# Expert blocks of 32 rows in four column quarters instead of 64 rows in two halves

## What is computed

```
expert_idx, gate_w = route(x2, w_router, router_bias)      # two experts of one group of four
h = silu(xb @ w1[e]) * (xb @ w3[e])                         # 1024 -> 512, xb: rows of expert e
y = h @ w2[e]                                               # 512 -> 1024
out[token] += gate * y                                      # summed over the token's two experts
```

## Time and profile before

| | us |
|---|---|
| runs | 3816.04, 3819.41, 3820.52 (median 3819.41) |
| profiled execution | 3819.16 |
| its span, first to last instruction | 3817.6 |
| TensorE matmuls busy | 3498.3 (92%), 15780 instructions |
| TensorE weight loads busy | 1803.3 (47%) |
| VectorE busy | 1159.3 (30%) |
| ScalarE busy | 757.9 (20%) |
| GpSimd busy | 177.0 (5%) |

### The profile page before, as it was taken

How to read it: one execution, slowest core, us unless ns; L and a number is a source line. 1 busy time by engine, 2 the same in 40 slices (tenths; PEclk the granted TensorE clock), 3 DMA queues, 4 the chain that set the end, 5 groups by cost and what they waited for, 6 DMA issues and landing times. The chain is left out here.

```text
span 3817.6 us, 47479 instructions
## 1 busy us (share of the span) xinstructions
PE 3498.3 (92%) x15780; PEld 1803.3 (47%) x15780; DVE 1159.3 (30%) x2400; ACT 757.9 (20%) x1418; POOL 177.0 (5%) x169
## 2 busy tenths in 40 slices
PE   8998998899969989997999679999998788899998
PEld 5445444555544454445555334444344577444443
DVE  1564112322333751113332320000446555410001
ACT  1134112223221151102222220000123422100000
POOL 1000002100020000003000110000000000000000
PEclk9999999899979999998999889999999887999999
DMA  7112223898231103234986212235121000122221
GB/s 280 56 45 78 77 77 132 324 389 353 77 130 66 56 23 112 76 133 153 420 336 268 81 57 77 77 83 143 67 76 54 1 0 0 44 77 77 77 77 66
DMA packets 79142, 457.64 MB, mean 120 GB/s; under 512 B 12160, under 2 KB 12296, under 8 KB 32112
## 3 DMA queue, kind: packets, MB, share of 16 engines
q1 hardware_dynamic: 42912, 310.40, 21.6%
q0 software_dynamic: 19776, 112.50, 8.3%
q10 hardware_dynamic: 16272, 32.43, 2.5%
HBM read 416.23 MB, written 39.06 MB: 119 GB/s over the span
## 5 line engine op out<-in xcount | busy, mean ns | idle before, releaser
L779 PE MATMUL pb<-arena,xT 128*64 x1984 | 445.6, 383 | 16.4 <-DVE streamed L1699 5.9
L779 PE MATMUL pb<-streamed,xT 128*64 128x256 f32 x1984 | 445.6, 383 | 0.0
L535 PE MATMUL pb<-xT,streamed 128*128 128x512 f32 x832 | 369.4, 603 | 0.0
L779 PEld LDWEIGHTS pb<-arena,xT 128*64 128x64 f32 x1984 | 267.8, 138 | 162.4 <-issue 31.6
L704 PE MATMUL pb<-xT,streamed 128*128 128x512 f32 x768 | 335.3, 595 | 2.6 <-ACT arena L1193 2.6
L888 PE MATMUL pb<-arena,streamed 128*128 128x512 f32 x704 | 306.4, 598 | 8.9 <-DMA streamed<-in_w_tail 7.2
L863 PE MATMUL pb<-xtok,streamed 128*128 128x512 f32 x704 | 305.0, 596 | 5.8 <-DVE xtok L1829 5.8
L863 PE MATMUL pb<-arena,streamed 128*128 128x512 f32 x704 | 304.2, 595 | 5.8 <-DVE arena L1829 5.8
L779 PEld LDWEIGHTS pb<-streamed,xT 128*64 128x64 f32 x1984 | 267.9, 138 | 0.0
L535 PEld LDWEIGHTS pb<-xT,streamed 128*128 128x128 f32 x832 | 159.9, 193 | 201.5 <-issue 201.4
L704 PEld LDWEIGHTS pb<-xT,streamed 128*128 128x128 f32 x768 | 146.4, 191 | 186.6 <-issue 186.6
(11 more groups left out here) (359 smaller groups left out, 3756.8 us busy)
## 6 DMA issues: line engine op xcount, KB each, us to landing
arena<-in_w_moe SPq DMA_DIRECT2D x128, 1024.0 KB, 11.7
streamed<-in_w_tail SPq DMA_DIRECT2D x87, 1024.0 KB, 4.8
streamed<-in_w_layer SPq DMA_DIRECT2D x78, 1024.0 KB, 4.9
arena<-in_w_moe POOLq DMA_DIRECT2D x64, 1024.0 KB, 9.7
ys_dram<-am ACTq DMA_DIRECT2D x120, 128.0 KB, 6.5
xT<-xs_dram ACTq DMA_DIRECT2D x26, 512.0 KB, 8.2
xs_dram<-lnw POOLq DMA_DIRECT2D x16, 512.0 KB, 20.5
lnw<-in_ln_par POOLq DMA_DIRECT2D x4, 1024.0 KB, 5.3
```

The lines of the kernel that those rows point to most:

```text
L535: last = mm(pb[bank][:, 0:cols], unit(w, u, k), rhs[:, k * cols:(k + 1) * cols], start=(k == 0), stop=(k == KC - 1))
L779: last = mm(pb[m][r0:r0 + MOE_BLOCK, 0:FW], rows, w, start=(k == 0), stop=(k == KC - 1))
```

## The change

MOE_BLOCK becomes 32. It follows that COLS = 4, FW = 128 and DW = 256 (columns of a part in up and down, before 256 and 512), N_BLK = (1024 + 16 * 31) // 32 = 47 and 12 tiles of four blocks in place of 16 of two. The relay buffers hold three of four parts, 3072 columns in place of 2048; w2's moves to another place. turn has one transpose in place of two. The three values per block become one, the expert's number, loaded ahead of silu (ScalarE) and of the hidden rows (VectorE); TensorE still loads its offset. One semaphore expert_here for each matrix replaces the two waits: SyncE and GpSimd wait for an expert's arrival and raise it. The copies of w1 and w3 no longer wait on up_ready themselves. The copy of the y block moves from VectorE to ScalarE, and its store is one DMA. TensorE's code is unchanged but for the sizes.

```diff
-MOE_BLOCK = 64
+MOE_BLOCK = 32
+STORES = 1
...
-        w2_relay = streamed[:, 2 * RELAY:3 * RELAY]
+        w2_relay = sr[:, 13312 - S - RELAY:13312 - S]
...
-        expert_loaded = [[sem(f"expert_loaded{q}_{p}") for p in range(PIECES // 2)] for q in range(2)]
+        expert_loaded = [sem(f"expert_loaded_{n}") for n in ("w1", "w3", "w2")]
+        expert_here = [sem(f"expert_here_{n}") for n in ("w1", "w3", "w2")]
...
-        def block_values(eng, b):
-            off = eng.value_load(blk_tab[0:1, b:b + 1], min_val=0, max_val=SLOT)
-            even = eng.value_load(blk_tab[0:1, N_BLK + b:N_BLK + b + 1], min_val=32, max_val=32 * N_EXP // 2)
-            odd = eng.value_load(blk_tab[0:1, 2 * N_BLK + b:2 * N_BLK + b + 1], min_val=32, max_val=32 * N_EXP // 2)
-            return off, even, odd
-        def wait_expert(eng, l, values, m):
-            for q in range(2):
-                eng.wait_ge(expert_loaded[q][m], l * (16 * N_EXP) + values[1 + q])
-                alone(eng)
+        def block_expert(eng, b):
+            return eng.value_load(blk_tab[0:1, N_BLK + b:N_BLK + b + 1], min_val=0, max_val=N_EXP - 1)
+        def slot_of(e):
+            return SLOT - (e & 1) * SLOT
...
@@ SyncE @@
+                def arrived(e, m):
+                    sp.wait_ge(expert_loaded[m], (l * N_EXP + e + 1) * 32)
+                    alone(sp)
+                    sp.sem_inc(expert_here[m], 1)
+                arrived(0, 0)
+                load_up(1, 0)
+                load_up(1, 1)
+                arrived(0, 1)
+                load_up(1, 2)
...
                 for e in range(2, N_EXP):
-                    for p in range(UP_PIECES):
-                        if p % 2:
-                            load_up(e, p)
-                            continue
-                        sp.wait_ge(expert_loaded[e % 2][p // 2], l * (16 * N_EXP) + 32 * (e // 2))
+                    for m in range(2):
+                        arrived(e - 1, m)
+                        sp.wait_ge(up_ready, l * (2 * N_BLK) + 2 * end + 1 + m)
                         alone(sp)
-                        sp.wait_ge(up_ready, l * (2 * N_BLK) + 2 * end + 1 + p // 2)
-                        alone(sp)
-                        load_up(e, p)
+                        load_up(e, 2 * m)
+                        load_up(e, 2 * m + 1)
+                for m in range(2):
+                    arrived(N_EXP - 1, m)
...
@@ GpSimd, expert loop; its arrived(e) is the same with w2's semaphores @@
+                    arrived(e - 1)
                     pool.wait_ge(y_ready, l * N_BLK + end + 1)
                     alone(pool)
-                    pool.wait_ge(expert_loaded[e % 2][2], l * (16 * N_EXP) + 32 * (e // 2))
-                    alone(pool)
                     for p in range(UP_PIECES, PIECES):
                         load_down(e, p)
...
@@ ScalarE @@
-                def relay_w1(b):
-                    values = block_values(act, b)
-                    wait_expert(act, l, values, 0)
-                    act.wait_ge(up_ready, 2 * (l * N_BLK + b) + 1)
+                def relay_w1(b, e):
+                    act.wait_ge(expert_here[0], l * N_EXP + e + 1)
                     alone(act)
-                    fn(cut(w1_relay, D_EXP - FW), cut(arena[:, bass.ds(values[0], KC * D_EXP)], D_EXP)[:, :, FW:D_EXP], ACT.Copy).then_inc(w1_relayed, 1)
+                    fn(cut(w1_relay, D_EXP - FW), cut(arena[:, bass.ds(slot_of(e), KC * D_EXP)], D_EXP)[:, :, FW:D_EXP], ACT.Copy).then_inc(w1_relayed, 1)
...
+                def copy_y(b):
+                    act.wait_ge(y_ready, l * N_BLK + b + 2)
+                    alone(act)
+                    act.wait_ge(y_stored[b % 2], 16 * STORES * (l * OUT_OF + b // 2) + 1)
+                    alone(act)
+                    fn(ysb[b % 2], pb[2 + b % 2][:, 0:DW], ACT.Copy).then_inc(y_copied, 1)
                 def store_y(b):
                     act.wait_ge(y_copied, l * N_BLK + b + 3)
                     alone(act)
-                    for g in range(COLS):
-                        act.dma_start(ys_dram[b * MOE_BLOCK:(b + 1) * MOE_BLOCK, g * DW:(g + 1) * DW],
-                                      ysb[b % 2][g * MOE_BLOCK:(g + 1) * MOE_BLOCK, :]).then_inc(y_stored[b % 2], 16)
+                    act.dma_start(ys_dram[b * MOE_BLOCK:(b + 1) * MOE_BLOCK, :].rearrange("r (g c) -> g r c", g=COLS),
+                                  ysb[b % 2]).then_inc(y_stored[b % 2], 16)
...
                 for b in range(N_BLK):
+                    if b + 1 < N_BLK:
+                        e = block_expert(act, b + 1)
                     gate_half(b)
                     if b + 1 < N_BLK:
-                        relay_w1(b + 1)
+                        relay_w1(b + 1, e)
...
+                    if b >= 1:
+                        copy_y(b - 1)
                     copy_hT(b)
                     if b >= 1:
                         store_y(b - 1)
+                copy_y(N_BLK - 1)
...
@@ VectorE; its copy_y goes, the tables of even and odd waits go, one of the block's expert comes @@
                 for b in range(N_BLK):
+                    if b + 1 < N_BLK:
+                        ahead = block_expert(dve, b + 1)
                     hidden(b)
...
-                    ahead = relay_w3(b + 1) if b + 1 < N_BLK else None
-                    if b >= 1:
-                        copy_y(b - 1)
-                    relay_w2(b, values)
+                    if b + 1 < N_BLK:
+                        relay_w3(b + 1, ahead)
+                    relay_w2(b, e)
```

More of the change, by code:

```diff
@@ L135, in two_blocks @@
         dest = sb("dest", 2 * NT, I32)
-        blk_tab = sb("blk_tab", 3 * N_BLK + N_EXP, I32)
+        blk_tab = sb("blk_tab", 2 * N_BLK + N_EXP, I32)
         gate2 = sb("gate2", 2 * NT)
@@ L375, in _ @@
                 load_up(0, 3)
-                for p in range(3):
-                    load_up(1, p)
+                def arrived(e, m):
[7 more added lines that the diff above has]
+                load_up(1, 2)
                 sp.wait_ge(mix_ready, (l + 1) * 8)
@@ L456, in _, with arrived @@
                 scale_rows(2 * l)
+                def arrived(e):
+                    pool.wait_ge(expert_loaded[2], (l * N_EXP + e + 1) * 32)
+                    alone(pool)
+                    pool.sem_inc(expert_here[2], 1)
                 pool.wait_ge(mix_ready, (l + 1) * 8)
                 alone(pool)
+                arrived(0)
                 for p in range(UP_PIECES, PIECES):
@@ L478, in _ @@
                 for e in range(2, N_EXP):
-                    end = pool.value_load(blk_tab[0:1, 3 * N_BLK + e - 2:3 * N_BLK + e - 1], min_val=0, max_val=N_BLK)
+                    end = pool.value_load(blk_tab[0:1, 2 * N_BLK + e - 2:2 * N_BLK + e - 1], min_val=0, max_val=N_BLK)
+                    arrived(e - 1)
                     pool.wait_ge(y_ready, l * N_BLK + end + 1)
-                    alone(pool)
-                    pool.wait_ge(expert_loaded[e % 2][2], l * (16 * N_EXP) + 32 * (e // 2))
                     alone(pool)
@@ L485, in _ @@
                         load_down(e, p)
-                for m in range(PIECES // 2):
-                    pool.wait_ge(expert_loaded[0][m], (l + 1) * (16 * N_EXP))
+                arrived(N_EXP - 1)
+                for m in range(2):
+                    pool.wait_ge(expert_here[m], (l + 1) * N_EXP)
                     alone(pool)
                 for s in range(2):
-                    pool.wait_ge(y_stored[s], 16 * COLS * OUT_OF * (l + 1) + 1)
+                    pool.wait_ge(y_stored[s], 16 * STORES * OUT_OF * (l + 1) + 1)
                     alone(pool)
@@ L1670, in _ @@
                 dve.drain()
-                c_off, c_even, c_odd = (r_tab[:, c * N_BLK:(c + 1) * N_BLK] for c in range(3))
                 v.tensor_scalar(r_half, r_blk, 0.5, -0.25, ALU.mult, ALU.add)
-                v.tensor_scalar(c_off, r_blk, -float(SLOT), float(SLOT), ALU.mult, ALU.add)
-                v.tensor_copy(r_tab[:, 3 * N_BLK:], r_end)
+                v.tensor_scalar(r_tab[:, 0:N_BLK], r_blk, -float(SLOT), float(SLOT), ALU.mult, ALU.add)
+                v.tensor_copy(r_tab[:, N_BLK:2 * N_BLK], r_blk)
+                v.tensor_copy(r_tab[:, 2 * N_BLK:], r_end)
                 dve.drain()
@@ L1677, in _ @@
                 dve.drain()
[L1678 to L1682 removed]
+                v.scalar_tensor_tensor(out=r_tab[:, 0:N_BLK], in0=r_half, scalar=2.0 * SLOT, in1=r_tab[:, 0:N_BLK], op0=ALU.mult, op1=ALU.add)
                 dve.drain()
@@ L1734, in _, with relay_w2 @@
                 dve.drain()
-                def relay_w2(b, values):
-                    wait_expert(dve, l, values, 2)
+                def relay_w2(b, e):
+                    dve.wait_ge(expert_here[2], l * N_EXP + e + 1)
+                    alone(dve)
                     dve.wait_ge(y_ready, l * N_BLK + b + 1)
                     alone(dve)
-                    src, out = values[0] + UP_PIECES * PAIR, cut(w2_relay, D - DW)
```

(10 more changed lines are left out.)

34 lines of the change are left out of this document (10 added, 24 removed).

## The result

The changed kernel takes 3893.37 us (median of 4 runs, 3886.68 to 3896.54) against 3819.6 for the kernel before in the same comparison: a ratio of 1.0193, 95% interval 1.0175 to 1.021. It is slower, where 3709 was forecast, and outside the range. The profiled execution has a span of 3895.0 us.

A forecast was written before the change was run, and what follows sets the result against it. TensorE's streaming was taken as the bound, expert loading close behind. The expert stage's 733.0 us becomes 312.5 + 305.3 = 617.8 (-115.2), +5 at the edges: -110, so 3709 us; forecast band 3690 to 3725, range 3672 to 3790.

The forecast's parts named there:

- T = 6.2 us a block: TensorE's 32-row block: up 3.70, down 1.73, turn and gaps 0.50, tile transposes 0.29; 6.2 us against 11.44.
- quarters take turns: Rival on TensorE: a quarter's weight load can't hide behind its matmul; up 6.7, block 9.25 us, total 3965; chance 0.11.
- two issues become one; hidden: ScalarE's y stores: two issues of 0.5 us each per block become one, behind the hT copy, costing nothing.
- The ring over w1: Last w1 pass, silu, ScalarE's next w1 copy, TensorE's start: 3.8 us, hidden behind TensorE's 4.08 us of other work.
- The rival of 6.7 to 7.6 us a block: Longer block period, from the register operation or a late w1 copy: total 3739 to 3811 us; chance 0.18.
- Loading the experts: Expert weights by DMA, 16.5 us an expert: waits of 19.1 us in layer 0 and 11.9 in layer 1.
- the prediction's own rules: Load e+2 begins when e is over and load e+1 landed; e+2 may start 3.2 us before its load completes.
- Ring over w3: Hidden rows, VectorE's next w3 copy, TensorE's start: 2.9 us against 4.4 of other TensorE work, so hidden.
- register loads: On the copying engines: three loads and two computed waits, 2.15 us on VectorE, become one load passing during waiting.
- Edges: Outside the expert stage: longer routing tables, four sums a tile at layer end; 2.5 us a layer, +5 in all.
- the lower bound: Up on TensorE: halves over 128 columns come every 54.5 ns; four quarters at that pace give 3.49 us.
- The extreme by 81 ns: Worst case on TensorE, 81 ns a matmul: an estimated 13.8 us a block, total 4380; no chance of its own.

The follow-up runs named there:

- 4: The changed kernel with TensorE's blocks 1 to 44 as a loop of 11 passes over four blocks, single buffers for rows and transpose: 3821.5 us.
- experiment 7: The changed kernel with TensorE in a loop and y stored in four DMAs a block, y still copied by ScalarE: 3764.4 us.
- experiment 9: The changed kernel with y stored in four DMAs a block in place of one, without the loop: 3904.8 us.
- experiment 12: The changed kernel with loop and four stores, y copied by ScalarE, leaving out seven eighths of the weights of experts 2 to 15: 3734.0 us.
- 6: The changed kernel with TensorE in a loop and y stored in four DMAs a block, y copied by VectorE: 3777.0 us.
- 5: The changed kernel with 64-row blocks and a block's y stored in two DMAs in place of one: 3818.7 us.
- 2: The kernel before with 32-row blocks and w2's relay buffer moved, keeping the old chains of the copying engines: 3990.1 us.
- experiment 8: The kernel before with each up matmul of 256 columns cut into four of 64: 4078.8 us.

## Why the prediction was wrong

The 184 us between 3709 and 3893 split in the order in which the faults were removed: the supply of instructions, 72 (change against 4); the store on four DMA engines, 57 (4 against 7), which comes out only once the first is gone; and 55 between experiment 7 and the forecast, of which some 26 are the loop's own turns. In the other order the four stores alone cost 11 more (change against 9), and the loop then gives 140 (9 against 7).

**The step that failed is "T = 6.2 us a block", the sum of what TensorE streams.** The terms that it has were right: in experiment 7 the 64 pairs of a w1 or w3 half start within 1.65 to 1.68 us when nothing stops them, so a pair every 26.2 to 26.7 ns, and half follows half after 1.77 us (up: 3.70 forecast, 3.5 measured); the quickest blocks of the change are 5.6 to 5.8 apart. What was missing is a term for the instructions. I noted that they double per block, and weighed it only as the cover of the weight loads. The kernel before consumes a packet each 373.4/25 = 14.9 us; at T the change needs one each 291/65 = 4.5 us, and gets one each 6.1 in the mean (6.2 beside the loads). Once the loads are over it takes one each 4.5 to 5.0 us, but for one of 6.4, with a single stop over 0.5 us from "issue" (1.8). The 100 packets of q8 on the page and the 25 in the stage could have been read beforehand; that the supply has a limit, and where, no row of before showed.

- **The rival "quarters take turns"**, which had 0.11, predicted the sign by a mechanism that isn't there. In experiment 7 the passes stand 0.108 to 0.110 us apart, with the four quarters starting within 26 ns, as the forecast asked for. By the 81 ns of the Trainium skill (TensorE: Matmul & The Clock Gate, Back-to-back issue gap) its up-projection alone would take an estimated 10.4 us (128 x 81 ns); its steady blocks are 5.6 to 8.2 in all.
- **Stores: "two issues become one; hidden"** priced the issue and not the transfer; the issue too was low, 0.5 us forecast and 1.02 measured in the changed kernel. It held in the changed kernel (experiment 9) only because of the larger loss; alone, with 64 rows, it costs 136 us.
- **The ring over w1, "hidden by 0.3 us only"**, is a part of what remains, and not the largest. Experiment 7's steady block is 6.7 where T was 6.2, 94 x 0.5 = 47 us. Without its stops it would be under T, since the streaming was overpriced; the three stops of each four blocks, 1.3 at the loop's turn, 1.2 for the copy of w1 and 0.5 for the rows, put 0.75 us on each. So the ring costs 22 us over both layers. Silu stands behind four store issues, 1.7 to 2.0 us where the forecast had one of 0.5, which is more than the 0.6 that it had to spare. The rival of 6.7 to 7.6 us a block named this place, and its 3739 at 6.7 was near; but the 6.7 was in part luck, since more of it is made by the loop than by the ring. Leaving out the turns, an estimate from experiment 7 (3764 - 26) is 3738.
- **Loading the experts**: 19.1 + 11.9 = 31.0 us forecast for both layers, 31.3 measured (7 against 12). The agreement is in part luck: by the prediction's own rules the waits shrink when a block takes 6.7 us, to 14 in both layers (stage 328 + 320, less 94 x 6.7 and twice the 2 of the start), so the loads cost about twice what the rules give at the pace that experiment 7 had, and experiment 12 still has an eighth of them. The page after shows the relayed semaphores late by 32.6 us before ScalarE's copies, but TensorE's waits for that copy are 5.2 us in layer 0.
- **Ring over w3, VectorE, register loads**: the y copy's move to ScalarE was forecast at nothing and gained 13 us where it was tried (6 against 7). The register and semaphore edits by themselves: 0 with 64 rows (5), 97 together with the store and y edits in 32-row blocks (2 against the change), 85 without the store edit (2 against 9).
- **Edges**: +5 forecast, +2.3 measured outside the stage.
- A slip without effect: the lower bound's (17.5 - 16 x 0.28)/240 is 54.3 ns, not 54.5. The extreme by 81 ns sums to about 4390 rather than 4380.

Open: why a packet takes 6 us beside the loads when it moves in 1 (queueing behind load packets, or being asked for late) was not separated; how much the single buffers of the looped kernels cost; and in experiment 7 the first blocks of a layer, in which the loop's body is fetched (6 packets in the first three distances of layer 0), still take 7.9 to 13.1 us.

## What to carry to other kernels

Count the instructions an engine needs per microsecond beside those it streams: the queue of instruction packets on the page gives it, and an edit that cuts work into smaller pieces multiplies it. Here straight code passes quietly where it needs one packet in 9 us, and stops TensorE where it needs one in 5.7 (experiment 8) or 4.5 (the change), while the DMA engines are full of loads. A loop over the same body removes most of that, at a price of 1.3 us a turn. And a DMA is priced by the dimension that is split over the engines, not by its number: joining four into one can take twelve of sixteen engines away from it.

## What the runs showed that was not expected

- One and the same TensorE program ran at 351 matmuls in 20 us beside 321 GB/s of DMA and at 516 beside 26 GB/s, both at a granted clock of 1.00, with no wait for another engine in either.
- A loop body of four blocks, some 1,430 instructions by the records, is fetched once a layer: 10 packets in the whole stage for 47 blocks.
- A turn of such a loop (a branch and two register loads) leaves TensorE idle for 1.3 us, 26 us in experiment 7.
- Pairs of load and matmul with four quarters beside each other keep 26.2 to 26.7 ns over 64 pairs at 128 columns; with two halves, a pair of 64 columns comes at 37 ns where half of a 128-column one would be 27.
- A store over two DMA engines backs up ScalarE's queue so far that the issue of the next DMA takes 9.55 us.
- The first fault hid the second: removing the slow store alone made the kernel 11 us slower, removing it after the other made it 57 us faster.
